# Two-layer decoder step: front reordered, gate from its own mixed tokens, three quarters of the first output product from rounded parts

## The reference, cut to what matters

```
a = rmsnorm(x) @ w_qkv_a              # 1024 -> 384 (q) + 256 (latents) + 64 (rotary key)
c_q, c_kv = rmsnorm(a_q), rmsnorm(a_kv);  q = c_q @ w_q_b;  attention, 8 heads of 128
h = x + o @ w_o                       # o: 8 heads x 128: "the first output product"
h = h + relu(rmsnorm(h) @ w_up)^2 @ w_down            # 4096 wide
n = rmsnorm(h);  xx = n_prev - n                      # layer 2, RWKV-7
xr, xk, xv, xg, ... = n + xx * mu[j]
r, k, v = xr @ w_r, xk @ w_k, xv @ w_v;  g = sigmoid(xg @ gw1) @ gw2
```

## Time and profile before

| | us |
|---|---|
| median of 3 runs | 3260.03 (3259.24 to 3260.14) |
| profiled execution | 3262.27 |
| its span in the trace | 3260.50 |
| PE busy | 3123.1 (96%) |
| DVE busy | 1850.3 (57%) |
| ACT busy | 1346.5 (41%) |
| POOL busy | 1256.1 (39%) |

### The profile page before, as it was taken

How to read it: one execution, slowest core, us unless ns; L and a number is a source line. 1 busy time by engine, 2 the same in 40 slices (tenths; PEclk the granted TensorE clock), 3 DMA queues, 4 the chain that set the end, 5 groups by cost and what they waited for, 6 DMA issues and landing times.

```text
span 3260.5 us, 69934 instructions
## 1 busy us (share of the span) xinstructions
PE 3123.1 (96%) x25708; PEld 2868.1 (88%) x25708; DVE 1850.3 (57%) x3160; ACT 1346.5 (41%) x2813; POOL 1256.1 (39%) x877
## 2 busy tenths in 40 slices
PE   8999999999999999999999999998999899999998
PEld 7788887788999999998899878787878799999998
DVE  4566663236444577765303477778735644458885
ACT  4244445413544433322224355566522344443332
POOL 0000000023766777722232122332224376677771
PEclk9999999999999999999999999999999999999999
DMA  3222225401544544431223201100251255454442
GB/s 114 57 77 75 73 61 175 150 13 56 162 158 156 185 128 144 144 99 54 78 80 115 73 21 34 40 28 27 48 171 36 64 163 159 154 182 146 145 133 78
DMA packets 307310, 330.47 MB, mean 101 GB/s; under 512 B 54366, under 2 KB 289809, under 8 KB 306994
## 3 DMA queue, kind: packets, MB, share of 16 engines
q1 hardware_dynamic: 301218, 308.64, 29.8%
q0 software_dynamic: 5904, 19.21, 1.9%
HBM read 232.05 MB, written 116.16 MB: 107 GB/s over the span
## 4 chain that ended last, share of the span: by engine, by line
PE 73%; DVE 10%; PEld 6%; issue 3%; POOL 3%; ACT 3%; DMA 1%; DVEq 0%; SPq 0%; PEldq 0%; ACTq 0%; POOLq 0%
PE bank L666 70%; PEld bank L666 6%; PE bank L674 4%; DVE arena L3812 1%; DVE hT L3883 1%; POOL wloA L2190 1%; POOL arena L2190 1%; POOL wloS L2190 1%; DVE arena L3502 1%; DVE arena L3215 1%; DVE arena L3373 1%; DVE arena L3513 0%; DVE std L3212 0%; DVE arena L3829 0%; DVE arena L3385 0%
## 5 line engine op out<-in xcount | busy, mean ns | idle before, releaser
L666 PE MATMUL bank<-arena 64*128 64x128 f32 (+18 forms) x7102 | 865.4, 310 | 36.8 <-DVE hT L3883 12.9
L666 PEld LDWEIGHTS bank<-arena 128*128 128x128 f32 (+10 forms) x7102 | 682.1, 164 | 192.9 <-issue 37.9
L2418 ACT COPY arena<-bank 128x512 f32<-128x512 f32 (+14 forms) x518 | 230.5, 485 | 593.6 <-PE bank L666 392.1
L2190 POOL TENSOR_TENSOR arena<-arena 128x512 f32<-128x512 f32 x120 | 164.7, 1372 | 475.3 <-PE bank L666 249.9
L2681 ACT ACTIVATE whiS<-arena 128x512 fp32r<-128x512 f32 x180 | 113.0, 628 | 406.5 <-POOL arena L2190 393.4
L2190 POOL TENSOR_TENSOR wloA<-arena,whiA 128x512 fp32r<-128x512 f32 x180 | 261.4, 1466 | 5.2 <-ACT whiA L2678 5.2
L2190 POOL TENSOR_TENSOR wloS<-arena,whiS 128x512 fp32r<-128x512 f32 x180 | 239.6, 1345 | 49.4 <-ACT whiS L2681 49.4
L3678 DVE TENSOR_TENSOR hT<-hT,bank 128x536 f32<-128x536 f32 x280 | 197.4, 706 | 82.7 <-PE bank L666 82.3
L674 PE MATMUL bank<-table,arena 128*128 128x128 f32 (+5 forms) x1422 | 181.8, 269 | 33.1 <-DVE arena L3385 13.0
L666 PE MATMUL bank<-hiT,whiS 128*128 128x268 f32 x768 | 199.3, 288 | 6.4 <-DVE loT L3517 3.7
L3522 DVE TENSOR_TENSOR arena<-std,bank 128x268 f32<-128x268 f32 x192 | 80.4, 431 | 218.1 <-PE bank L666 208.9
(11 more groups left out here) (346 smaller groups left out, 8678.4 us busy)
## 6 DMA issues: line engine op xcount, KB each, us to landing
u_scratch<-arena SPq DMA_DIRECT2D x480, 134.0 KB, 1.9
arena<-in_ffn_w_up SPq DMA_DIRECT2D x64, 512.0 KB, 4.2
arena<-u_scratch SPq DMA_DIRECT2D x56, 536.0 KB, 5.0
arena<-in_ffn_w_down SPq DMA_DIRECT2D x112, 256.0 KB, 3.9
arena<-u_scratch SPq DMA_DIRECT2D x56, 402.0 KB, 5.8
arena<-past_scratch SPq DMA_DIRECT2D x32, 640.0 KB, 7.3
past_scratch<-in_cache_kv_latent SPq DMA_DIRECT2D x128, 128.0 KB, 2.4
past_scratch<-in_cache_k_rope SPq DMA_DIRECT2D x128, 32.0 KB, 2.2
```

Source lines behind the costliest of these rows:

```text
L666: return pe.matmul(out, lhsT, rhs, start=first, stop=last, skip_group_check=group)
L2190: return pool.tensor_tensor(out, a, b, op)
L2418: lane.do(act.copy(dst, b if view is None else view(b)), ring.drained)
```

## The change

1. **Front.** The twelve row loads are issued by ACT at its start and no longer by SP. PE turns the rows after tiles 0 to 2. `down_first` runs over the 8 weight rows outside and the 3 tiles inside. ACT squares tokens ahead of rounding piece 1; `down(1, 0)` stands ahead of `spread_scales(1)`; the sums of squares stand earlier among the `down` products, with buffers of their own for the latents' deviations. The raw queries of pieces 0 and 1 stand ahead of the last norm and of the meeting of all engines.
2. **Gate.** DVE mixes tokens for the gate too (`MIXED = r, gate, k, v`), and PE multiplies these by `w_g` once: 8 float32 matmuls for each piece and not 16. The weights `mu * w_g` of the gate fall away.
3. **First output product.** Quarters 1 to 3 take seven heads from rounded parts and the eighth in float32. ACT rounds seven rows of the weights and the heads of three quarters, DVE splits them (partly in place of the weights themselves); the first weight blocks of the feed-forward part lie in the same memory, so that ACT's rounding of them and POOL's splits now come at the end of quarter 3.

```diff
@@ PE, front
-                for n, cols in enumerate(tiles):
-                    held.append(rv.bank(ahead=n))
-                    for j in range(KT):
-                        if n == 0:
-                            pe.wait_ge(whi_s, j + 1)
+                for j in range(KT):
+                    pe.wait_ge(whi_s, j + 1)
+                    for n, cols in enumerate(tiles):
                         mm(held[n][:, 0:w], wa_hi[:, j, cols], token_hi[0][:, j, :], j == 0, False)
-            turn_tiles(range(0, 6))
+            turn_tiles(range(0, 3))
             pe.wait_ge(rows_s, 192)
...
-            turn_tiles(range(6, 9))
+            turn_tiles(range(3, 9))
...
+            down(1, 0)
             spread_scales(1)
-            down(1, 0)
             down(2, 0)
...
-            latent_tiles(range(5, NQ + 1))
+            latent_tiles(range(4, NQ + 1))
...
+            raw_query(0)
+            raw_query(1)
             norm_t.expect()
             pe.wait_ge(norm_s, norm_t.n)
             meet(pe, here)
+            raw_query(2)
@@ PE, out_product_0
+                q = [l * TH + s * TS for s, l in QUARTERS].index(at)
+                if q == 1:
+                    pe.wait_ge(wlo_s, FRONT_W + 3 + k // 2 + 1)
+                if k == 0:
+                    pe.wait_ge(xlo_s, FRONT_X + q)
+                b = rv.bank()
+                for j in range(OUT_R):
+                    mm(b[:, 0:w], wo_hi[j][:, cols], out_hi[q][:, j, :], j == 0, False)
+                    mm(b[:, 0:w], wo_hi[j][:, cols], out_lo[:, j, at:at + w], False, False)
+                for j in range(OUT_R):
+                    mm(b[:, 0:w], wo_lo[j][:, cols], out_hi[q][:, j, :], False, False)
+                rv.done(mm(b[:, 0:w], wo[1][:, H - 4, cols], oT[:, H - 1, at:at + w], False, True))
@@ PE, gate
-            pe.wait_ge(mu_s, 2)
             for p in range(3):
-                b = ra.bank()
-                lora_sums(b, w_g, nT, p, True, False)
-                ra.done(lora_sums(b, w_mu, DX, p, False, True))
+                pe.wait_ge(xm_s, mixed_before("gate") + p + 1)
+                ra.done(lora_sums(ra.bank(), w_g, x_mix, p, True, True))
+                through(xu_t)
@@ POOL, feed
+                fold_quarter(0)
+                fold_quarter(1)
...
-                weights_of(0, None, unused)
...
+                    first_sums()
                 fold_quarter(2)
                 fold_quarter(3, (0, 4))
+                if layer == 0:
+                    pool.wait_ge(v_drained, mark["adds0"] + 4 * KT)
+                    first_splits()
+                    fourth(0, None, unused)
@@ ACT, feed
+                if layer == 0:
+                    round_out_weights(range(3))
+                    round_heads(1)
+                    act.wait_ge(wo_s, 16)
+                    round_out_weights(range(3, OUT_R))
+                    round_heads(2)
...
                 squares_at(3, (7, KT))
+                if layer == 0:
+                    for name in ("A11", "S3", "S2", "S1"):
+                        round_weights(0, name, unused)
                 round_block("21", 0)
+                if layer == 0:
+                    round_weights(0, "A12", unused)
                 round_block("T4", 0)
+                if layer == 0:
+                    round_weights(0, "A22", unused)
                 deviations_at(3)
@@ DVE, feed
-                    adds(0, *range(KT))
-                    adds(1, *range(KT))
+                    split_out_rows()
+                    adds(0, 0)
+                    split_heads(1)
+                    for pair in range(4):
+                        adds(0, *range(2 * pair + (pair == 0), 2 * pair + 2))
+                        split_out_columns(pair)
+                    split_heads(2)
+                    adds(1, *range(4))
+                    split_heads(3)
+                    adds(1, *range(4, KT))
@@ DVE, mixed tokens
-                    dve.wait_ge(lora_used, 1)
-                    dve.wait_ge(wl_s, 48)
-                    dve.tensor_tensor(w_mu[:, :, :], w_g[:, :, :], prm[...].broadcast_to([P, KT, P]), ALU.mult).then_inc(mu_s, 1)
+            for p in range(3):
+                mixed("gate", p)
+            for m, name in ((1, "k"), (2, "v")):
+                mixed(name, 0)
+                mixed(name, 1)
+                split_mixed(m, 0)
+                mixed(name, 2)
+                split_mixed(m, 1)
+                split_mixed(m, 2)
```

More of the change, by code:

```diff
@@ L379, in program @@
         wo = [Carve(past_at + at * NPG * (KVL + ROPE))(n, D) for at, n in ((2, 3), (0, 5))]
+        assert past_at == 25936 and past_at + 2 * NPG * (KVL + ROPE) == 36176
         class Feed:
@@ L401, in __init__ @@
                 late = [tile(at[name], 4, TH)[:, :, TS:TH] for name in ("T4", "T2")]
-                whole = [tile(at[name], KT, TS) for name in ("T4", "T2", "raw")]
+                whole = [tile(at[name], KT, TS) for name in ("T4", "T2")] + [self.fb[:, 0, :, TS:TH] if at is FEED_AT[0] else tile(at["raw"], KT, TS)]
+                t1 = self.lo32["T1"]
+                self.first_sums = {"S3": t1[:, :, TS:TS + P], "S1": t1[:, :, TS + P:TS + 2 * P]} if at is FEED_AT[0] else {}
                 self.sq = [[sq[:, k, :] for k in range(KT)] for sq in whole] + [[late[k // 4][:, k % 4, :] for k in range(KT)]]
@@ L642, in program, with mixed_before @@
         u_d = nc.dram_tensor("u_scratch", (NG, 8, P, TH), F32).ap()
+        MIXED = ("r", "gate", "k", "v")
+        def mixed_before(name):
+            return 3 * MIXED.index(name)
         def meet(eng, here):
@@ L833, in _ @@
             pe.wait_ge(xlo_s, 3)
-            for k in range(3, 6):
-                down(k, 2)
-            latent_sums("kv_squares1", kv_sq[1])
+            down(3, 2)
+            latent_sums("q_squares1", q_sq[1])
+            down(4, 2)
+            down(5, 2)
             down(0, 2)
+            latent_sums("kv_squares2", kv_sq[2])
             rv.wait_drained(1)
@@ L1115, in out_product_0 @@
             def out_product_0(at, w, k):
-                first = 3 if at == 0 else 0
-                product(rv, lambda j: (wo[0][:, first + j] if first + j < 3 else wo[1][:, first + j - 3])[:, k * P:(k + 1) * P],
-                        lambda j: oT[:, first + j, at:at + w], H - first, w=w)
+                cols = slice(k * P, (k + 1) * P)
+                if at == 0:
+                    product(rv, lambda j: wo[1][:, j, cols], lambda j: oT[:, 3 + j, 0:TS], 5, w=w)
+                    return
+                q = [l * TH + s * TS for s, l in QUARTERS].index(at)
[10 more added lines that the diff above has]
+                rv.done(mm(b[:, 0:w], wo[1][:, H - 4, cols], oT[:, H - 1, at:at + w], False, True))
             added(0, out_product_0)
@@ L2508, in _ @@
             deviations_of_tokens(2)
+            scales_out(1)
             act.wait_ge(fin_sq, FRONT_SQ)
@@ L2680, in round_weights @@
                         sum_b[layer].wait(act, c, summed)
-                        ins = act.activation(hi[name][:, :, :], s2t if name == "S2" else lo32[name], ACT.Copy)
+                        src = s2t if name == "S2" else lo32[name]
+                        if layer == 0 and isinstance(c, int) and c == 0 and name in f.first_sums:
+                            src = f.first_sums[name]
+                        ins = act.activation(hi[name][:, :, :], src, ACT.Copy)
                     ins.then_inc(wh_b[layer].sem, 1)
@@ L2729, in feed, with round_out_weights, round_heads @@
                     deviations_at(1)
-                for name in ("A11", "S3", "S2", "S1", "A12", "A22", "S4"):
-                    round_weights(0, name, unused)
+                def round_out_weights(rows):
+                    for j in rows:
+                        act.activation(wo_hi[j], wo[0][:, j] if j < 3 else wo[1][:, j - 3], ACT.Copy).then_inc(whi_s, 1)
+                def round_heads(q):
+                    s, l = QUARTERS[q]
+                    at = l * TH + s * TS
+                    act.activation(out_hi[q], oT[:, 0:OUT_R, at:at + TS], ACT.Copy).then_inc(xhi_s, 1)
+                if layer == 0:
[4 more added lines that the diff above has]
+                    round_heads(2)
+                else:
+                    for name in ("A11", "S3", "S2", "S1", "A12", "A22", "S4"):
+                        round_weights(0, name, unused)
                 act.wait_ge(norm_s, norm_t.n)
@@ L2734, in feed @@
                     squares_at(0)
+                    round_heads(3)
                     squares_at(1)
@@ L2739, in feed @@
                     round_block(name, 0)
-                wl_b[layer].wait(act, 0)
+                if layer == 1:
+                    wl_b[layer].wait(act, 0)
                 squares_at(2)
@@ L2750, in feed @@
                 round_block("22", 0)
+                if layer == 0:
+                    round_weights(0, "S4", unused)
                 round_block("11", 1)
@@ L3589, in feed @@
                 dve.wait_ge(scaled_s, 4 * layer + 4)
```

(10 more changed lines are left out.)

184 lines of the change are left out of this document (106 added, 78 removed).

## The result

| | before | after |
|---|---|---|
| median, us | 3259.64 (3255.86 to 3260.77, 6 runs) | 3242.31 (3235.95 to 3251.35, 6 runs) |
| profiled execution | 3262.27 | 3241.11 |
| its span | 3260.5 | 3239.3 |

The ratio is 0.9949, with an interval from 0.9936 to 0.9963: 17 us faster, where 30 were forecast. The forecast of 3230 missed by 12; the time lies within the range (3219 to 3243).

A forecast was written before the change was run, and what follows sets the result against it. The chain of waits, 79% PE and its weight loads, was taken as the bound. Front 15.9, gate 8.1 and output product 5.8 sum to 29.8 us: 3232.5 profiled, 3230 median, range 3219 to 3243 (8 times in 10).

The forecast's parts named there:

- Front, start: Kernel start: without row loads between, weights land at 22.7 and PE starts at 23.3, not 25.75; 2.4 us gained.
- First group: Front's first 24 `down` matmuls: going along with ACT's eight roundings, they take 6.1 instead of 7.6 us; 1.5 gained.
- the way to the last `down`: Front, later `down` products: second scales in time gain 4.4, a late sum of squares loses 0.5, piece 2 gains 0.9 us.
- Tail: Front, last `down` to rotation: 14.2 us instead of 21.4, raw queries computed beside DVE's norm; 7.2 gained.
- All later work, SP's page gathers too, hangs on the same meeting and moves along: Behind the front: everything later, gathers included, shifts with the front's gain of 15.9 us.
- Output product: First output product: 24 results at 3.05 instead of 3.61 us gain 13.4; less two stalls, net 5.8.
- rival 4: Output product: rounded matmuls don't run at 0.124 us but 0.25 each, 60 us lost, time 3304; chance 0.03.
- Stall (a): Output product, sum of quarter 2's squares: PE asks before POOL is done; 2.3 us lost, bounds 0 and 5.
- Stall (b): Output product's end: ACT's roundings and POOL's weight operations beside DVE's chain cost 5.3 us, bounds 2.5 and 10.
- rival 2: Output product gives all back: full contention and quarter 2's sum with a clock drop, 13.4 - 5 - 9; 3236, chance 0.17.
- Gate: Gate: half its 48 float32 matmuls fall away, 14.3 us, less 3.7 idle and 2.5 half clock; net 8.1.
- rival 1: Front keeps only 8 us, as moved sums bring one or two more waits of over 2 us; 3238, chance 0.21.

The follow-up runs named there:

- e11: The changed kernel with gathers split 24, 35, 35, 34, but the twelve row loads issued by SP ahead of the first weights: 3239.30 us.
- e2: The kernel before, with SP's page gathers split 36, 32, 30, 30 over the head pairs: 3271.33 us (+10.6).
- e5: Only the gate part of the change, on the kernel before: 3251.50 us (-8.3).
- e6: Only the first output product's part of the change, on the kernel before: 3252.78 us, ratio 0.9983 (0.9971 to 0.9995).
- e3: Only the front part of the change, on the kernel before: 3253.49 us (-7.2).
- e4: Only the front part, on the kernel before, with gathers split 24, 35, 35, 34: 3242.69 us (-18.0).
- e13: The changed kernel run once more with the same code, beside the kernel with early gathers on the same chip: 3243.09 us.
- e1: The changed kernel with SP's page gathers split 24, 35, 35, 34 over the head pairs instead of 32 each: 3236.48 us.
- e7: The changed kernel with gathers 24, 35, 35, 34 and, in layer 0, ACT's squares of quarter 2 ahead of rounding T3 and T1: 3232.32 us.

## Why the prediction was wrong, step by step

**Front, start (2.4 forecast, 0.8 in the trace, none on the whole): mis-sized.** The weights that ACT scales first were asked for 3.1 us sooner (SP's requests for weights begin at 6.91 instead of 10.03; the tokens' took 0.5 longer to issue) and took 3.6 us longer: they landed at about 24.2, not at 23.7 as before or 22.7 as forecast. The expectation of `e11` says 3.6 sooner, which is wrong by this half. DMA issues of the kernel after (KB, us to landing); they answer to the earlier trace rows:

```profile
arena<-in_mla_w_qkv_a SPq DMA_DIRECT2D x1, 256.0 KB, 16.8
...
arena<-in_x_sample SPq DMA_DIRECT2D x1, 128.0 KB, 13.2
```

I had counted on getting the poor stretch of the earlier trace rows back. It is still there (stages of the kernel after), at 244 GB/s instead of 300:

```profile
15.80:19.50 3.70, 3.33 (x20) 3.09 (x19) 1.72 (x3) 1.76 (x3) 0.00 (x0) 0.70 1.02 244
```

It was not the rows' stretch: the rows had landed by 12.47, when PE turned them. The last tokens landed later too, at 6.44 + 13.2 = 19.6 instead of 16.9; the prediction had named a delay of the tokens as a sign of being wrong. The 0.8 of the trace has another source than the landing. Before, ACT was copying tiles until 25.00 and only then scaled the weights; now it stands ready and scales them at 24.20, as they land. Even this is within the scatter. The first product started at 24.3, 25.0, 25.8 and 26.2 in four traces with the old start, and from 24.7 to 25.9 in eleven with the new one: the starts of one kernel differ by more than the step was to bring. The Trainium skill (DMA: Bandwidth & Descriptors, Issuing engines are not separate DMA queues) says that only issue time is saved; the trace agrees, and shows that here the issue time saved was worth nothing for the start.

**First group (1.5) and the way to the last `down` (4.8): 5.0 of the 6.3.** 24.96 to 39.68 is 14.7, against 16.5: 1.8. The wait for the second scales is gone; the sums are at 48.00 without a wait, where the earlier trace rows had 2.43. From there to the last `down` 3.2 were gained instead of 4.8, some of it lost in sums that come close upon their results (one wait of 0.66).

**Tail (7.2): right in these two traces, and partly by luck.** 131.31 - 109.89 = 21.4 became 118.38 - 104.12 = 14.3, so 7.1. The norm was ready at 8.2 and two raw queries over at 11.7 (7.8 and 11.6 forecast). But the 21.4 that the forecast was read from is high: `e2`, `e5` and `e6`, with the same front, took 19.3 to 19.7. The 18 rows of raw queries took 7.34 before at a granted clock of 0.78, and 5.64 in `e5` and `e6` at 1.00. Against these three the tail gained 5.0 to 5.5. The front gave 12.9 of 15.9 in the two traces; over four traces with the old front and eleven with the new and with rows by ACT, the mean start of the rotation is 129.4 and 118.1, which is 11.3.

**"All later work, SP's page gathers too, hangs on the same meeting and moves along": this step failed.** It is two errors in one. The rotation moved by 12.9, but the meeting only by 7.4 (page table at 115.88 instead of 123.24), because the change takes two raw queries out from behind the meeting; SP begins its gathers 6.9 sooner (133.32 to 126.42), they run at their own pace (81.9 us for 32, 80.9 before), and the weights are asked for 5.9 sooner. And I had not looked how late SP already was: the row of 215.72 with its 5.3 of landing shows 0.3 us of slack. 12.9 - 5.9 - 0.3 is the wait of 6.7; the half clock behind it adds 2.1. 9.0 of the front's 12.9 went there. The prediction reckoned SP's queue only for the weights of pair 0.

**Output product: results right, both stalls too small.** 24 results gave 13.7 (3.06 each in quarter 1, 3.03 later; 3.05 forecast, so rival 4 was far off). Stall (a) cost 5.2 instead of 2.3: 3.63 of waiting, and the product behind it took 4.65 instead of 3.03. ACT's squares waited in line behind two roundings, which the prediction didn't follow. Stall (b) cost 6.2 instead of 5.3: from the last add to the seventh product 18.0 us instead of 11.7. 3.07 of it is POOL beside DVE, which is more than the 2.6 forecast for all of POOL; 2.1 is ACT's roundings ahead of block 21 (forecast 2.7 for all of ACT's), and the rest a second split stretched from 1.27 to 2.04 and a wait of 0.24. Quarter 0 took 21.3 instead of 20.1 for the same work, its clock granted 0.86 instead of 0.92 of full; this is scatter and not the change, for only `e6` shows it again, and nine other traces with part 3 took 19.9 to 20.1. 13.7 - 5.2 - 6.2 - 1.3 leaves 0.9 (1.0 by the rounded terms); forecast 5.8. Without the scatter of quarter 0 it would be 2.2. The term that was missed most is stall (a), which came at rival 2's 5 with rival 2's clock drop; stall (b) was nearer to its forecast of 5.3 than to rival 2's 9. The Trainium skill (GPSIMD Engine Reference, Key points) speaks of contention for DVE instructions with two SBUF inputs, and gives no factor. The trace agrees, with 1.9 times for the eight products by the norm, but only those that POOL really meets are stretched, 3.35 of the chain's 8 us and one split; the prediction's doubling of the whole chain did not come.

**Gate (8.1): right, 8.2.** PE's timeline of the kernel after; it answers to the earlier trace rows:

```profile
1585.88 5.40 PE L685 MATMUL bank<-x_mix,std 128*128 128x384 f32 x16 [0.38 <-issue]
...
1604.72 0.42 PE L685 MATMUL bank<-x_hi,w_hi 128*128 128x384 f32 x1 [3.18 <-DVE x_lo L3887]
```

18.84 instead of 28.68; then ten matmuls at 0.32 instead of 0.18 cost 1.6. The idle time was 3.2 (3.7 forecast), the clock 1.6 (2.5), and the three pieces took 15.7 with their small gaps (14.3). Alone it brought 8.3.

**Sum.** Instructions with a name give 12.9 - 9.0 + 0.9 + 8.2 = 13.0. The other 8.2 of the traces' 21.2 lie where nothing was changed: 1.2 in the sample attention, 3.8 from the first group to the gate, 3.1 behind it. Much of that is scatter: from the first group to the gate `e3`, `e4` and `e5`, whose code there is the old one, took 816.2 to 817.7 us, the kernel after 816.2, and only the profiled execution before 820.1. But the medians keep 17.3 (17.6 for `e13`), some 4 more than 13.0, and `e4` and `e6` too did better in the median than their instructions account for. What these 4 us are I can't tell from traces that scatter by as much; it stays open. (13.0 still lies in the interval of the result, which spans 12.1 to 20.9 us, and not in that of `e13`, 0.9930 to 0.9955.)

**The rivals.** The time lies near rivals 1 and 2 together, 3244. That is luck as far as rival 1 goes: its reason, sums in the front for which PE waits over 2 us, was not there (one wait of 0.66). What took the front's gain was SP's queue, which no rival named.

## What to carry to other kernels

An engine that only issues DMAs has a schedule too. Before moving a stage forward, take the requests that its engine makes during it, and subtract landing time from use: a wait of zero in the profile can mean a slack of next to zero (0.3 us here). If a loop of small transfers stands ahead of a large one that someone will need, put the large one where its buffer comes free, and let the small ones fill the rest. And where work is shifted on to GpSimd beside a chain of VectorE, ask which of VectorE's instructions it will meet: here those with two SBUF inputs took 1.9 times as long while they met it.

## What was not expected of the hardware

The same wait doesn't always cost the same. PE waits 1.17 us in the sample attention of every kernel here; twelve matmuls of the same size behind it took, among others, 2.96, 4.43 or 5.71 us, at a mean granted clock of 1.00, 0.67 and 0.50 of full: the clock stayed full, or fell to its half level for a part or for all of them. `e1`, the kernel after and `e7`, timelines of PE:

```profile
618.22 0.39 PE L685 MATMUL bank<-arena,table 128*128 128x4 f32 x2 [1.17 <-DVE arena L3539]
618.46 2.96 PE L685 MATMUL bank<-arena 128*128 128x268 f32 x12
```
```profile
628.99 0.59 PE L685 MATMUL bank<-arena,table 128*128 128x4 f32 x2 [1.17 <-DVE arena L3539]
629.44 4.43 PE L685 MATMUL bank<-arena 128*128 128x268 f32 x12
```
```profile
620.37 0.59 PE L685 MATMUL bank<-arena,table 128*128 128x4 f32 x2 [1.17 <-DVE arena L3543]
620.82 5.71 PE L685 MATMUL bank<-arena 128*128 128x268 f32 x12
```

The part from the end of the heads to the output product so takes 130.1, 131.8 or 133.1 us in the traces, with the same code in this part; why the clock fell in one and not in another is not shown. Other stretches scatter too: from the gate to the end kernels with the new gate took 1653.4 to 1663.4. The runs of most kernels here spread by 5 to 17 us. The clock fits that: of the six runs of the kernel after, the fastest (3235.95) had a mean granted clock of 0.990 and the slowest (3251.35) one of 0.987. That it is the only cause isn't shown. Either way one trace can't carry a claim of 3 us unless it names the instructions.
